# A diffusion backbone kernel: its beginning ordered by token tile instead of by column pair

## The chip, the cores and the metric

The program runs on one core of a Trainium2 chip, in one launch. The metric is the device time of one execution in microseconds (us), median over runs. All data are float32.

## The reference

Two layers over 256 latent tokens x and 256 context tokens, width 2048. Only the beginning of layer 0 matters here:

```
mod = silu(c) @ ada_w[0] + ada_b[0]            # shift, scale, gate, shift2, scale2, gate2, each 2048 wide
h_lat = rms_norm(x, norm_mix_g[0]) * (1 + scale) + shift
h_ctx = rms_norm(ctx, norm_mix_g[0]) * (1 + cscale) + cshift     # the same with silu(c_ctx)
q, k, v = h_lat @ attn_w_qkv                   # 2048 x 3072: 16 query heads, 4 key and 4 value heads of 128
k_c, v_c = h_ctx @ attn_w_qkv[:, 2048:]
```

Behind it follow grouped-query attention with rotary angles, the output projection, a squared-ReLU MLP (2048 to 8192 to 2048), and a second layer with a Fourier mixer and a second MLP.

## The kernel before

**Precision.** TensorE multiplies float32 operands in a reduced form, so each operand is split in two: a high half (`w_hi`, `h_hi`) written by ScalarE as a copy to that form, and a low half (`w_lo`, `h_lo`), written by VectorE as the difference. A product is three matmuls: high x high, low activation x high weight, high activation x low weight (`three`).

**Weights.** SP issues transfers of 1 MB ("pieces") into a ring `raw` of three. A piece is two slices; slice s is split by `split_hi(s)` on ScalarE (L712) and `split_lo(s)` on VectorE (L1197) into one of four slots (s % 4). A slot can be written again when its products are done: `slot_used` (L95) gives the number of products to wait for. The first three pieces cover two tiles of 128 rows of the weights (the K direction) and 1024 output columns each: slice 2p holds K tile 0 and slice 2p+1 K tile 1 of piece p.

**Products.** `product(r)` on TensorE (L1855) is one output block of 128 tokens x 512 columns over the K tiles of its group. `product_at(r)` (L106) gives (piece, column block, token tile). The first eight products are in the order (0,0,0), (0,0,1), (0,1,0), (0,1,1), (1,2,0), (1,2,1), (1,3,0), (1,3,1): both token tiles of a column block behind each other, so piece 0 serves products 0 to 3 and piece 1 products 4 to 7. Products 8 to 15 use piece 2, the last four for context tokens. Results are copied out of the banks by ScalarE (`first_copy`) or, for five of them, VectorE (`copy_first`).

**Modulation.** Two of the 16 column tiles of shift and scale are needed first. POOL issues the first four modulation transfers of 1 MB into `spare`; TensorE multiplies each (`first_piece`, 16 matmuls), ScalarE copies the rows (`rows_out(0)`), TensorE turns them to columns (`first_cols(0)`, 8 matmuls), VectorE adds bias and gain (`take_first(0, 0)`). The further modulation pieces wait until the context has landed (`load_start(4)`, L646).

**x.** ScalarE's queue issues both tiles of x, 128 tokens x 2048 each. ScalarE squares them (`square_in`), takes the root (`root_in`), VectorE normalises (`normed_in`) into `xn_in`. TensorE turns `xn_in` by 128 x 128 transposes. `turn_input(i)` turns column tiles 2i and 2i+1 of both token tiles into one bank (four transposes), and `x_out(i)` copies it to `xT`; numbers 0 to 5 come before the first product, 6 and 7 behind product 1. `shape(0, 0)` on ScalarE scales and shifts column tiles 0 and 1 for both token tiles and writes `h_hi`, `lower(0, 0)` on VectorE writes `h_lo`.

**Order.** Each engine executes its own list in order; semaphores join them, and there is no scheduler. ScalarE's list from the first copy on (L844 to L870) is: x_out 0, 1, rows_out(0), split 0, shape(0, 0), split 1, x_out 2 to 5, split 2, x_out 6, 7, first_copy 0, 1, split 3, first_copy 3, splits 4 and 5, then the squares of the two context tiles with their roots and first_copy(4) between them. TensorE turns the context's first columns (`turn_ctx(0)`) behind product 9. SP waits for the second modulation piece (L587) before it issues weights 0, 1, the context (2 MB) and weights 2.

Of the kernel before, what the change touches and what calls it, by code (L numbers as in the profile page):

```python
# [94 lines left out]
def slot_used(s):  # L95

    p = s // 2
    return products_before(p + 1) if p < 23 else 80
# [7 lines left out]
def product_at(r):  # L106

    p = max(p for p in range(24) if products_before(p) <= r)
# [20 lines left out]
X_BANK = (0, 1, 2, 3, 4, 5, 4, 5)  # L129
# [115 lines left out]
def layer_block(nc, x, c, ctx_in, c_ctx, ada_w, ada_b, norm_mix_g, norm_mlp_g, w_qkv, q_g, k_g, w_o,  # L245
# [125 lines left out]
    x_in = sem("x_in")  # L371
# [178 lines left out]
    def _(sp):  # L550
# [36 lines left out]
        sp.wait_ge(ada_in[start_slot(1)], 16)  # L587
        for p in range(24):
            if p < 6:
                load_first(p)  # L590
            else:
                load_columns(p, wqkv_v[p // 6, column_block(p)])
# [48 lines left out]
    def _(pool):  # L641
# [53 lines left out]
        for n in range(19):  # L695
            load_start(n)
# [14 lines left out]
    def _(act):  # L711
# [22 lines left out]
        for tt in range(2):  # L734
            act.dma_start(x_tm[:, tt, :], x[0, tt * P:(tt + 1) * P, :]).then_inc(x_in, 16)
# [8 lines left out]
        def square_in(st):  # L744

            if st < 2:
                act.wait_ge(x_in, 32)
# [3 lines left out]
            for b in range(4):  # L751
# [11 lines left out]
        for st in range(2):  # L763
            square_in(st)
            root_in(st)
        def x_out(i):

            act.wait_ge(x_T, i + 1)
            act.activation(xT[:, 2 * i:2 * i + 2, :], ps[:, X_BANK[i], :].rearrange("p (a t) -> p a t", a=2),
                           ACT.Copy).then_inc(x_T_out, 1)  # L770
# [23 lines left out]

        def first_copy(r):
# [4 lines left out]
            if r == 0:  # L800
                act.wait_ge(x_T, 8)
# [41 lines left out]

        x_out(0)  # L844
        x_out(1)
        rows_out(0)
        split_hi(0)
        shape(0, 0)
        split_hi(1)
        x_out(2)  # L850
        x_out(3)
        x_out(4)
        x_out(5)
        split_hi(2)
        x_out(6)
        x_out(7)
        first_copy(0)
        first_copy(1)
        split_hi(3)
# [336 lines left out]
    def _(dve):  # L1196
# [156 lines left out]

        def add_product(r):
# [70 lines left out]
        total_in(1)  # L1425
        normed_in(1)
# [5 lines left out]
        lower(0, 0)  # L1432
        split_lo(1)
        take_first(0, 1)
        split_lo(2)
        copy_first(2)
        split_lo(3)
# [405 lines left out]
    def _(pe):  # L1843
# [11 lines left out]
        def product(r):  # L1855
# [3 lines left out]
            if r < 5:  # L1859
                pe.wait_ge(x_T_out, (1, 2, 3, 4, 7)[r])  # L1860
            elif r == 33:
                pe.wait_ge(ctx_T_out, 7)
            else:
                pe.wait_ge(*flushed(bank_before(r)))
            hi, lo = (h_hi, h_lo) if tt < 2 else (hc_hi, hc_lo)
            pe.wait_ge(h_ready, 2 * c + 1 + tt // 2)
# [241 lines left out]
        def turn_input(i):  # L2108

            pe.wait_ge(xn_made, 3 + i // 4)  # L2110
            if i >= 6:
                pe.wait_ge(x_T_out, i - 1)
# [342 lines left out]
```

## Time and profile before

| what | value |
|---|---|
| median of three runs | 2008.24 us |
| lowest, highest | 2007.26, 2008.89 us |
| the profiled execution | 2007.61 us |
| its span, first to last instruction | 2005.8 us |
| TensorE busy | 1967.7 us, 98% |
| mean granted TensorE clock | 0.996 |
| VectorE, ScalarE busy | 1386.6, 969.4 us |
| HBM read | 535.91 MB |

The times in a profile count from the first instruction. A time line or a chain of waits gives start and duration; a bracket behind an instruction says how long its engine had been idle and what ended it. PE is TensorE's matmul, PEld its weight load, DVE VectorE, ACT ScalarE, POOL GpSimd. L numbers are lines of the kernel.

### The profile page before, as it was taken

The page shows a single profiled execution, that of the slowest core. Times are in us where ns is not written, and L with a number is a line of the kernel's source. Part 1 is how long each engine was busy: PE and PEld are TensorE (multiplying, and loading weights), DVE is VectorE, ACT ScalarE, POOL GpSimd, SP SyncE. Part 2 cuts the span into 40 slices and gives each one's busy share as a digit, 9 for nine tenths or more (in the row PEclk, how much of TensorE's full clock was granted, in tenths as well). Part 3 has the DMA queues.
Part 4 walks back from the last instruction along what each step waited for, and adds up shares of the span by engine and source line. Part 5 has one row for each costly group of instructions (what it writes and reads, how often), then busy time and mean ns, then how long its engine had stood idle before and what let it go on. Part 6 is the DMA issues. An engine that isn't in the chain of part 4 may idle for free.

```text
span 2005.8 us, 25016 instructions
## 1 busy us (share of the span) xinstructions
PE 1967.7 (98%) x10204; PEld 1609.2 (80%) x10204; DVE 1386.6 (69%) x1420; ACT 969.4 (48%) x1265; POOL 111.1 (6%) x196
## 2 busy tenths in 40 slices
PE   6999999999999999999999999999999999999998
PEld 4677756778888888888888788788888888888886
DVE  3666898879868787788878775766666455555456
ACT  6432565445544445544444454555554454444444
POOL 1111001100000000000000000000000000000000
PEclk9999999999999999999999999999999999999999
DMA  9998768769989899799999726577776566555653
GB/s 358 338 379 315 278 257 295 287 237 324 358 288 353 314 363 354 271 363 365 357 354 359 273 85 190 175 249 253 257 250 223 185 196 210 189 192 196 221 189 126
DMA packets 152261, 542.80 MB, mean 271 GB/s; under 512 B 9393, under 2 KB 10577, under 8 KB 114641
## 3 DMA queue, kind: packets, MB, share of 16 engines
q1 hardware_dynamic: 119312, 335.77, 47.7%
q0 software_dynamic: 31744, 201.34, 27.2%
q10 hardware_dynamic: 1090, 4.09, 0.5%
q8 instruction: 81, 1.33, 0.3%
q14 instruction: 34, 0.28, 0.0%
HBM read 535.91 MB, written 2.10 MB: 268 GB/s over the span
## 4 chain that ended last, share of the span: by engine, by line
PE 92%; DVE 3%; DMA 2%; ACT 1%; issue 1%; POOL 0%; ACTq 0%; DVEq 0%; POOLq 0%
PE ps L2098 13%; PE ps L2032 11%; PE ps L2036 11%; PE ps L2035 11%; PE ps L2096 11%; PE ps L2099 6%; PE ps L1848 6%; PE ps L2095 6%; PE ps L1849 5%; PE ps L1850 5%; PE ps L2257 1%; PE ps L2204 1%; PE ps L1913 1%; DMA spare<-in_ada_w 1%; PE ps L2242 1%
## 5 line engine op out<-in xcount | busy, mean ns | idle before, releaser
L1201 DVE TENSOR_TENSOR w_lo<-raw,w_hi 128x1024 fp32r<-128x1024 f32 x616 | 749.3, 1223 | 472.2 <-ACT w_hi L727 472.0
L727 ACT ACTIVATE w_hi<-raw 128x1024 fp32r<-128x1024 f32 x616 | 649.2, 1059 | 848.1 <-PE ps L2036 345.8
L2098 PE MATMUL ps<-hh,w_hi 128*128 128x512 f32 x1088 | 426.9, 398 | 1.7 <-DVE hh L1627 1.7
L2032 PE MATMUL ps<-w_hi,hh 128*128 128x512 f32 x992 | 386.1, 389 | 1.5 <-DVE w_lo L1201 1.5
L2035 PE MATMUL ps<-w_lo,hh 128*128 128x512 f32 x992 | 386.0, 389 | 0.0
L2036 PE MATMUL ps<-w_hi,hh 128*128 128x512 f32 x992 | 385.9, 389 | 0.0
L2096 PE MATMUL ps<-hh,w_hi 128*128 128x512 f32 x960 | 379.9, 396 | 0.0
L2099 PE MATMUL ps<-hh,w_lo 128*128 128x256 f32 x1088 | 302.8, 278 | 0.0
L2095 PE MATMUL ps<-hh,w_lo 128*128 128x256 f32 x960 | 267.5, 279 | 0.0
L2099 PEld LDWEIGHTS ps<-hh,w_lo 128*128 128x128 f32 x1088 | 205.3, 189 | 40.8
L2032 PEld LDWEIGHTS ps<-w_hi,hh 128*128 128x128 f32 x992 | 186.2, 188 | 40.5 <-DVE w_lo L1201 1.9
L2036 PEld LDWEIGHTS ps<-w_hi,hh 128*128 128x128 f32 x992 | 186.2, 188 | 38.8
L2035 PEld LDWEIGHTS ps<-w_lo,hh 128*128 128x128 f32 x992 | 186.2, 188 | 38.5
L2098 PEld LDWEIGHTS ps<-hh,w_hi 128*128 128x128 f32 x1088 | 206.9, 190 | 11.6 <-issue 5.5
L2095 PEld LDWEIGHTS ps<-hh,w_lo 128*128 128x128 f32 x960 | 180.2, 188 | 43.7
L1229 DVE SCALAR_TENSOR_TENSOR ada_sum<-ada_raw,silu,ada_sum 128x2048 f32<-128x2048 f32 x83 | 194.7, 2346 | 2.0 <-DMA ada_raw<-in_ada_w 1.9
L1848 PE MATMUL ps<-w_hi,hh 128*128 128x512 f32 x448 | 191.2, 427 | 3.1 <-DVE hh L1351 1.6
L2096 PEld LDWEIGHTS ps<-hh,w_hi 128*128 128x128 f32 x960 | 180.0, 187 | 0.0
L1849 PE MATMUL ps<-w_lo,hh 128*128 128x512 f32 x448 | 175.8, 392 | 0.0
L1850 PE MATMUL ps<-w_hi,hh 128*128 128x512 f32 x448 | 175.2, 391 | 0.0
L693 POOL DMA_DIRECT2D ada_raw<-in_ada_w x132 | 70.9, 537 | 1150.6 <-DVE ada_sum L1229 586.0
L1848 PEld LDWEIGHTS ps<-w_hi,hh 128*128 128x128 f32 x448 | 84.5, 189 | 38.6 <-issue 13.9
(252 smaller groups left out, 1618.4 us busy)
## 6 DMA issues: line engine op xcount, KB each, us to landing
raw<-in_mlp_w SPq DMA_DIRECT2D x256, 1024.0 KB, 5.4
ada_raw<-in_ada_w POOLq DMA_DIRECT2D x151, 1024.0 KB, 6.0
spare<-in_ada_w POOLq DMA_DIRECT2D x29, 1024.0 KB, 7.0
raw<-in_attn_w_qkv SPq DMA_DIRECT2D x24, 1024.0 KB, 10.4
raw<-in_attn_w_o SPq DMA_DIRECT2D x16, 1024.0 KB, 7.7
raw<-in_fourier_w_o SPq DMA_DIRECT2D x16, 1024.0 KB, 5.1
g_row<-in_ada_w POOLq DMA_DIRECT2D x12, 1024.0 KB, 9.0
g_row<-gate_rows SPq DMA_DIRECT2D x48, 64.0 KB, 5.2
```

Of the source, the lines that this page charges most:

```text
L727: act.activation(w_slot(s)[0], raw[:, piece % RAW, s % 2, :], ACT.Copy).then_inc(hi_ready, 1)
L1201: nc.vector.tensor_tensor(lo, raw[:, s // 2 % RAW, s % 2, :], hi.bitcast(F32), ALU.subtract).then_inc(lo_ready, 1)
L1848: mm(dst, w_h, m_h, start=start, stop=False, skip_group_check=True)
L1849: mm(dst, w_h, m_l, start=False, stop=False, skip_group_check=True)
L1850: return mm(dst, w_l, m_h, start=False, stop=stop, skip_group_check=True)
L2032: ins = mm(bank_of(tt, nb), h_hi[:, k % KT, tok], hi[:, cols], start=start, stop=False)
L2035: mm(bank_of(tt, nb), h_hi[:, k % KT, tok], lo[:, cols], start=False, stop=False)
L2036: return mm(bank_of(tt, nb), h_lo[:, k % KT, tok], hi[:, cols], start=False, stop=stop)
L2095: mm(ps[:, bank, 0:T], w_lo[:, s % SPLIT, w], h_hi[:, k, :], start=False, stop=False, skip_group_check=True)
L2096: ins = mm(both, w_hi[:, s % SPLIT, w], hh[:, k, :, :], start=False, stop=(k == KT - 1), skip_group_check=True)
L2098: mm(both, w_hi[:, s % SPLIT, w], hh[:, k, :, :], start=(k == 0), stop=False, skip_group_check=True)
L2099: ins = mm(ps[:, bank, 0:T], w_lo[:, s % SPLIT, w], h_hi[:, k, :], start=False, stop=(k == KT - 1), skip_group_check=True)
```

## The change

The second tile of x is issued on POOL's queue behind the first four modulation transfers; each tile of x has a semaphore of its own. SP waits for the fourth modulation transfer before the first weights, and for the sixth before weights 3. x is turned by token tile: `turn_x_in(tt, j)` turns column tiles 4j to 4j+3 of one token tile; the first tile's four calls come behind modulation piece 1, the second tile's behind products 1 and 3. Shaping and low half are made by token tile too (`shape_first`, `lower_first`). Products 0 to 3 are the four column blocks of token tile 0, products 4 to 7 those of tile 1; slots 0 and 1 are free after six products. ScalarE's and VectorE's lists are reordered accordingly.

```diff
--- before.py
+++ after.py
@@ -95,6 +95,8 @@
 def slot_used(s):
 
     p = s // 2
+    if p == 0:
+        return 6
     return products_before(p + 1) if p < 23 else 80
 
 
@@ -105,6 +107,8 @@
 
 def product_at(r):
 
+    if r < 8:
+        return TILE_FIRST[r]
     p = max(p for p in range(24) if products_before(p) <= r)
     j = r - products_before(p)
     if p >= 6:
@@ -126,7 +130,12 @@
     return max(m for m in range(r) if product_bank(m) == product_bank(r))
 
 
-X_BANK = (0, 1, 2, 3, 4, 5, 4, 5)
+TILE_FIRST = ((0, 0, 0), (0, 1, 0), (1, 2, 0), (1, 3, 0), (0, 0, 1), (0, 1, 1), (1, 2, 1), (1, 3, 1))
+
+
+def turned_x_bank(tt, j):
+
+    return j if tt == 0 else (5, 7)[j % 2]
 
 
 def group_tiles(c):
@@ -368,7 +377,9 @@
     ada_in = [sem(f"ada_in{i}") for i in range(11)]
     c_in = sem("c_in")
     small_in = sem("small_in")
-    x_in = sem("x_in")
+    x_in = [sem(f"x_in{i}") for i in range(2)]
+    first_hi = sem("first_hi")
+    first_h = sem("first_h")
     ctx_rows_in = sem("ctx_rows_in")
     rope_in_sem = sem("rope_in_sem")
     dft_in_sem = sem("dft_in_sem")
@@ -584,8 +595,10 @@
                                  gate_rows[v != 0][32 * j:32 * j + 32, :]).then_inc(gate_in, 16)
 
         sp.dma_start(ident[:, :], ident_in).then_inc(c_in, 16)
-        sp.wait_ge(ada_in[start_slot(1)], 16)
+        sp.wait_ge(ada_in[start_slot(3)], 16)
         for p in range(24):
+            if p == 3:
+                sp.wait_ge(ada_in[start_slot(5)], 16 * start_count(5))
             if p < 6:
                 load_first(p)
             else:
@@ -692,7 +705,10 @@
                 pool.wait_ge(slice_done, 2 * P_DOWN[0] - QKV + 128)
             pool.dma_start(ring(vector_slot(i)), ada_v[lay][m, i % KT]).then_inc(ada_in[vector_slot(i)], 16)
 
-        for n in range(19):
+        for n in range(4):
+            load_start(n)
+        pool.dma_start(x_tm[:, 1, :], x[0, P:2 * P, :]).then_inc(x_in[1], 16)
+        for n in range(4, 19):
             load_start(n)
         load_vector(0)
         load_vector(1)
@@ -731,8 +747,7 @@
 
         act.dma_start(vec_rows[0:16, 3, :], c[0].rearrange("(t p) -> t p", p=P)).then_inc(c_in, 16)
         act.dma_start(vec_rows[16:32, 3, :], c_ctx.rearrange("(t p) -> t p", p=P)).then_inc(c_in, 16)
-        for tt in range(2):
-            act.dma_start(x_tm[:, tt, :], x[0, tt * P:(tt + 1) * P, :]).then_inc(x_in, 16)
+        act.dma_start(x_tm[:, 0, :], x[0, 0:P, :]).then_inc(x_in[0], 16)
         for l in range(2):
             act.dma_start(vec_rows[0:96, l, :], ada_b[l].rearrange("(t p) -> t p", p=P)).then_inc(small_in, 16)
         act.dma_start(vec_rows[0:32, 2, :], norm_mix_g.rearrange("l (t p) -> (l t) p", p=P)).then_inc(small_in, 16)
@@ -741,14 +756,14 @@
         act.activation(sig[:, :], misc[:, 0:32], ACT.Sigmoid).then_inc(sig_ready, 1)
         act.wait_ge(eps_set, 4)
 
-        def square_in(st):
+        def square_in(st, blocks=range(4)):
 
             if st < 2:
-                act.wait_ge(x_in, 32)
+                act.wait_ge(x_in[st], 16)
             else:
                 act.wait_ge(ctx_rows_in, 16)
             src = x_tm if st < 2 else c_rows
-            for b in range(4):
+            for b in blocks:
                 j = 4 * st + b
                 if j >= 2:
                     act.wait_ge(xs_done, j - 1)
@@ -760,14 +775,14 @@
             act.activation(rst_in[:, st, 1:2], rst_in[:, st, 0:1], ACT.Sqrt,
                            bias=eps_col[:, 1:2]).then_inc(xroot_ready, 1)
 
-        for st in range(2):
-            square_in(st)
-            root_in(st)
-        def x_out(i):
-
-            act.wait_ge(x_T, i + 1)
-            act.activation(xT[:, 2 * i:2 * i + 2, :], ps[:, X_BANK[i], :].rearrange("p (a t) -> p a t", a=2),
-                           ACT.Copy).then_inc(x_T_out, 1)
+        square_in(0)
+        root_in(0)
+
+        def x_out(tt, j):
+
+            act.wait_ge(x_T, 4 * tt + j + 1)
+            act.activation(xT[:, 4 * j:4 * j + 4, tt * P:(tt + 1) * P],
+                           ps[:, turned_x_bank(tt, j), :].rearrange("p (a t) -> p a t", a=4), ACT.Copy).then_inc(x_T_out, 1)
 
         def rows_out(c):
 
@@ -792,13 +807,23 @@
             act.wait_ge(mod_done, shaped[0])
             act.activation(dst[:, kts, :], src[:, kts, :], ACT.Copy).then_inc(hhi_ready, 1)
 
+        def shape_first(tt):
+
+            tok = slice(tt * P, (tt + 1) * P)
+            act.wait_ge(a_ready, 1)
+            act.wait_ge(x_T_out, 4 * tt + 1)
+            for kt in range(2):
+                act.activation(xT[:, kt, tok], xT[:, kt, tok], ACT.Identity, bias=mod_col[:, kt:kt + 1],
+                               scale=a_col[:, 0, kt:kt + 1]).then_inc(mod_done, 1)
+            shaped[0] += 2
+            act.wait_ge(mod_done, shaped[0])
+            act.activation(h_hi[:, 0:2, tok], xT[:, 0:2, tok], ACT.Copy).then_inc((first_hi, hhi_ready)[tt], 1)
+
         def first_copy(r):
 
             if r in FIRST_ON_VECTOR:
                 return
             p, cb, tt = product_at(r)
-            if r == 0:
-                act.wait_ge(x_T, 8)
             if r == 9:
                 act.wait_ge(ctx_T, 8)
             act.wait_ge(prod_done, r + 1)
@@ -841,22 +866,24 @@
                 dst = qT[:, 4 * b:4 * b + 4, tt * P:(tt + 1) * P]
             act.activation(dst, src, ACT.Copy).then_inc(head_T_out, 1)
 
-        x_out(0)
-        x_out(1)
+        for j in range(4):
+            x_out(0, j)
         rows_out(0)
+        square_in(1, range(2))
+        shape_first(0)
         split_hi(0)
-        shape(0, 0)
         split_hi(1)
-        x_out(2)
-        x_out(3)
-        x_out(4)
-        x_out(5)
+        square_in(1, range(2, 4))
+        root_in(1)
         split_hi(2)
-        x_out(6)
-        x_out(7)
+        x_out(1, 0)
+        shape_first(1)
+        x_out(1, 1)
+        split_hi(3)
         first_copy(0)
+        x_out(1, 2)
         first_copy(1)
-        split_hi(3)
+        x_out(1, 3)
         first_copy(3)
         split_hi(4)
         split_hi(5)
@@ -1351,6 +1378,13 @@
             nc.vector.tensor_tensor(lo[:, kts, :], src[:, kts, :], hi[:, kts, :].bitcast(F32),
                                     ALU.subtract).then_inc(h_ready, 1)
 
+        def lower_first(tt):
+
+            tok = slice(tt * P, (tt + 1) * P)
+            dve.wait_ge((first_hi, hhi_ready)[tt], 1)
+            nc.vector.tensor_tensor(h_lo[:, 0:2, tok], xT[:, 0:2, tok], h_hi[:, 0:2, tok].bitcast(F32),
+                                    ALU.subtract).then_inc((first_h, h_ready)[tt], 1)
+
         def add_product(r):
 
             p, cb, tt = product_at(r)
@@ -1422,19 +1456,20 @@
 
         total_in(0)
         normed_in(0)
-        total_in(1)
-        normed_in(1)
         for i, (dst, w) in enumerate(((bias_col[:, 0:96], 96), (bias_col[:, 96:192], 96), (misc[:, 32:96], 64))):
             dve.wait_ge(vec_T, 3)
             nc.vector.tensor_copy(dst, ps[:, 7, i * P:i * P + w]).then_inc(vec_ready, 1)
         take_first(0, 0)
         split_lo(0)
-        lower(0, 0)
+        lower_first(0)
         split_lo(1)
+        total_in(1)
+        normed_in(1)
+        split_lo(2)
+        lower_first(1)
+        split_lo(3)
         take_first(0, 1)
-        split_lo(2)
         copy_first(2)
-        split_lo(3)
         split_lo(4)
         split_lo(5)
         total_in(2)
@@ -1856,14 +1891,17 @@
 
             p, cb, tt = product_at(r)
             c = r // 16
-            if r < 5:
-                pe.wait_ge(x_T_out, (1, 2, 3, 4, 7)[r])
+            if r < 4:
+                pe.wait_ge(x_T_out, r + 1)
             elif r == 33:
                 pe.wait_ge(ctx_T_out, 7)
-            else:
+            elif r > 4:
                 pe.wait_ge(*flushed(bank_before(r)))
             hi, lo = (h_hi, h_lo) if tt < 2 else (hc_hi, hc_lo)
-            pe.wait_ge(h_ready, 2 * c + 1 + tt // 2)
+            if r < 4:
+                pe.wait_ge(first_h, 1)
+            else:
+                pe.wait_ge(h_ready, 2 * c + 1 + tt // 2)
             tok = slice((tt % 2) * P, (tt % 2 + 1) * P)
             kts = group_tiles(c)
             n = kts.stop - kts.start
@@ -2105,16 +2143,16 @@
         pe.wait_ge(silu_ready, 1)
         pe.wait_ge(ones_set, 1)
 
-        def turn_input(i):
-
-            pe.wait_ge(xn_made, 3 + i // 4)
-            if i >= 6:
-                pe.wait_ge(x_T_out, i - 1)
-            for k in range(2):
-                for tt in range(2):
-                    f = 2 * i + k
-                    ins = nc.tensor.transpose(ps[:, X_BANK[i], k * T + tt * P:k * T + (tt + 1) * P], xn_in[:, tt, f * P:(f + 1) * P],
-                                              ident[:, :])
+        def turn_x_in(tt, j):
+
+            pe.wait_ge(xn_made, 2 * tt + j // 2 + 1)
+            if (tt, j) == (1, 1):
+                pe.wait_ge(vec_ready, 3)
+            if tt == 1 and j >= 2:
+                pe.wait_ge(x_T_out, 3 + j)
+            for k in range(4):
+                f = 4 * j + k
+                ins = nc.tensor.transpose(ps[:, turned_x_bank(tt, j), k * P:(k + 1) * P], xn_in[:, tt, f * P:(f + 1) * P], ident[:, :])
             ins.then_inc(x_T, 1)
 
         first_piece(0)
@@ -2122,14 +2160,11 @@
         pe.wait_ge(small_in, 64)
         for i, n in enumerate((96, 96, 64)):
             nc.tensor.transpose(ps[:, 7, i * P:i * P + n], vec_rows[0:n, i, :], ident[0:n, 0:n]).then_inc(vec_T, 1)
+        for j in range(4):
+            turn_x_in(0, j)
         first_piece(2)
-        turn_input(0)
-        turn_input(1)
         first_piece(3)
-        turn_input(2)
         first_cols(0)
-        for i in range(3, 6):
-            turn_input(i)
 
         def turn_ctx(i):
 
@@ -2150,9 +2185,9 @@
 
         for r in range(77):
             product(r)
-            if r == 1:
-                turn_input(6)
-                turn_input(7)
+            if r in (1, 3):
+                turn_x_in(1, r - 1)
+                turn_x_in(1, r)
             if 9 <= r < 12:
                 turn_ctx(2 * r - 18)
                 turn_ctx(2 * r - 17)
```

## Rows read from the trace of the kernel before

**Rows 1.** The page: span, busy time of the engines, the chain by engine.
```profile
span 2005.8 us, 25016 instructions
...
PE 1967.7 (98%) x10204; PEld 1609.2 (80%) x10204; DVE 1386.6 (69%) x1420; ACT 969.4 (48%) x1265; POOL 111.1 (6%) x196
...
PE 92%; DVE 3%; DMA 2%; ACT 1%; issue 1%; POOL 0%; ACTq 0%; DVEq 0%; POOLq 0%
```

**Rows 2.** The chain of waits, 20 to 50 us: start us, us, what.
```profile
4.07 18.79 DMA spare<-in_ada_w
...
22.90 1.47 PE ps L1887 x16
...
26.34 0.17 DVE a_col L1321
...
32.20 0.43 PE ps L1848
...
36.23 0.23 PE ps L1849
...
38.58 2.00 ACT w_hi L727 x2
40.59 2.45 ACT sq_in L755 x8
...
44.04 2.46 ACT sq_in L755 x8
...
47.23 1.12 DVE c_rows L1309
...
48.40 1.09 PE ps L2146 x8
```

**Rows 3.** Busy time by stretch: bounds, length, engines, granted clock, transfers' share, GB/s.
```profile
0.00:15.00 15.00, 2.24 (x17) 0.87 (x17) 1.52 (x11) 5.04 (x11) 3.88 (x8) 1.00 0.85 298
15.00:20.00 5.00, 3.94 (x31) 1.65 (x35) 3.08 (x7) 3.35 (x11) 0.00 (x0) 1.00 1.03 350
20.00:25.00 5.00, 4.65 (x36) 2.51 (x28) 0.70 (x4) 1.79 (x4) 0.00 (x0) 1.00 1.02 394
...
31.00:34.00 3.00, 3.00 (x8) 2.33 (x8) 1.23 (x1) 1.12 (x2) 0.78 (x1) 0.52 1.01 406
```

**Rows 4.** TensorE in order of time: start us, us, instruction, [idle before].
```profile
20.67 1.97 PE L2116 MATMUL ps<-ident,xn_in 128*128 128x128 f32 x8
...
29.11 0.47 PE L1848 MATMUL ps<-w_hi,hh 128*128 128x512 f32 x1 [1.64 <-DVE hh L1351]
...
34.27 1.04 PE L2116 MATMUL ps<-ident,xn_in 128*128 128x128 f32 x8
...
39.23 0.50 PE L1848 MATMUL ps<-w_hi,hh 128*128 128x512 f32 x1 [0.49 <-DVE w_lo L1201]
```

**Rows 5.** Transfers issued at 15.77 and 16.71 us: count, size, us to landing.
```profile
raw<-in_attn_w_qkv SPq DMA_DIRECT2D x1, 1024.0 KB, 8.5
...
c_rows<-in_ctx SPq DMA_DIRECT2D x1, 2048.0 KB, 16.2
```

**Rows 6.** ScalarE by line and shape, 20 to 62 us: xcount | busy, mean ns.
```profile
L727 ACT ACTIVATE w_hi<-raw 128x1024 fp32r<-128x1024 f32 x8 | 8.4, 1059 | 0.0
...
L769 ACT ACTIVATE xT<-ps 128x512 f32<-128x512 f32 x8 | 4.3, 594 | 6.3 <-PE ps L2116 6.3
...
L789 ACT ACTIVATE xT<-xT,mod_col,a_col 128x256 f32<-128x256 f32 x2 | 1.1, 594 | 0.6 <-DVE a_col L1321 0.6
```

**Rows 7.** The same view, 200 to 300 us: halves of width 256 on ScalarE and VectorE.
```profile
L948 ACT ACTIVATE hh<-ps 128x256 fp32r<-128x256 f32 x4 | 1.5, 376 | 0.4 <-PE ps L2257 0.4
...
L1544 DVE TENSOR_TENSOR hh<-ps,hh 128x256 fp32r<-128x256 f32 x4 | 1.7, 418 | 0.0
```

**Rows 8.** VectorE by line and shape, 20 to 62 us.
```profile
L1201 DVE TENSOR_TENSOR w_lo<-raw,w_hi 128x1024 fp32r<-128x1024 f32 x8 | 9.7, 1221 | 2.7 <-ACT w_hi L727 2.7
...
L1309 DVE TENSOR_SCALAR xn_in<-x_tm,rst_in 128x1024 f32<-128x1024 f32 x1 | 0.7, 748 | 0.0
```

## The prediction

> **What bounds the kernel now.** I read the page first. The span is 2005.8 us, TensorE has work in 98% of it, and 92% of the chain that ended last is TensorE [rows 1]. So what is lost before its first products, or between them, is hardly won back later. The change touches only the first 60 us. There the chain of waits has two parts [rows 2]. Up to 22.9 us it is a transfer: the fourth piece of modulation weights (issued at 4.07, landed at 22.9). Then come its matmuls, the copy of the rows, the columns, the shaping of x and the halves of the first weights. Later, from 38.58 to 48.40, the chain leaves TensorE: ScalarE splits slices 4 and 5, squares the context's eight blocks, VectorE normalises, and at 48.40 TensorE can turn the context. That is 9.8 us from the first split, 7.8 from the end of the second (40.59). This second part is what the reader should hold on to: whatever starts split 4 later moves the turning by as much.
>
> The bytes come next [rows 3]: the transfers run at the full share from 4 us on, and they move 298 GB/s over the first 15 us, 350 up to 20 and 394 up to 25. Last, TensorE in order of time [rows 4]: eight transposes take 1.97 us at 20.67 and 1.04 at 34.27; the first product waits until 29.11; slice 3 costs only 0.49 us of waiting at 39.23.
>
> **The transfers.** One transfer is 1.05 MB. The fourth piece needs four pieces, one tile of x and 0.2 MB of small loads ahead of it: 5.4 MB. By rows 3, 4.47 MB are there at 15 us and 0.350 MB come per us, so it lands at about 17.8 (was 22.9); I take 18.2, because the second tile of x, which moved at a high rate, is no longer among these bytes. The second tile follows in the same queue: 6.5 MB, about 20.8. The SP queue now waits for the fourth piece and not for the second, so its first weights are issued at 18.2 and not at 15.8. Landing took 8.5 us from issue [rows 5], which would make 26.7; but ahead of that landing the same seven transfers are on the way as before, and by the sum of the bytes they are there at 24.3, as now. I take 24.3 and keep 26.7 as the upper end. The context (issued at 16.7, 16.2 us to landing [rows 5]: 32.9) stays, for the same reason. The piece at which SP now waits again before its fourth weights costs nothing: these weights are used behind the context's squares.
>
> The Trainium skill, "DMA: Bandwidth & Descriptors", section "Issuing engines are not separate DMA queues", says that transfers of all issuing engines run on the same 16 engines and interleave. By it, the new order can bring nothing forward of the bytes that the first weights stand behind: 24.3, and a t0 (below) of 27.1; by the row alone it would be 29.5. It speaks against much gain from the transfers.
>
> **Up to the first product.** TensorE turns the first tile (16 transposes) ahead of pieces 2 and 3; this takes 1.9 us at the faster pace of rows 4 and 3.9 at the slower, all while it waits for piece 3 anyway if the faster holds. From piece 3's first matmul (22.90) to the shaping factors (26.5) it was 3.6 us [rows 2]: factors at 21.8. ScalarE however has two blocks of the second tile's squares ahead of the shaping, waiting for that tile: 20.8 + 1.2 = 22.0. The shaping of half the width (two activations of 0.4, one copy of 0.38, by the 256 wide ones of 0.59 and 0.38 [rows 6, 7]) ends at 23.2. The first split waits for its weights: 24.3 + 1.05 = 25.35; low half + 1.22 [rows 8] = 26.6; the low half of h, 0.42 [rows 7], stands behind it in VectorE's order: t0, the first product, = 27.1, 2.0 earlier than 29.11. If TensorE is slow before, t0 is 28.1; with the late weights 29.5.
>
> **Two products, then a stall.** TensorE now stands idle from about 21.5 to 27.1. After an idle time of 1.6 us (with 0.5 more behind it) the granted clock was 0.52 in the stretch from 31 to 34 [rows 3], the level of 1.2 GHz: matmuls came every 0.43 us and not every 0.23 [rows 2], eight of them, 1.6 us lost. So I take nine of the first twelve at 0.43 and three at 0.23: products 0 and 1 end at 31.7. Only then does TensorE turn the first two quarters of tile 1. ScalarE stands in order behind that: quarter out (32.2 to 32.75, 0.59 each [rows 6], 0.5 in a stream), shaping of tile 1 (1.15), second quarter (0.5), and only then split 3 (1.05): 35.5; its low half on VectorE: 36.75. Product 2 needs slice 3 for its second half, since by tile it now comes after two products and not after four. TensorE has its transposes and product 2's first half done at 33.35 and waits 3.4 us, where it waited 0.49 before.
>
> Behind it are nine matmuls (products 2 and 3), eight transposes, and twelve matmuls (products 4 and 5). At 0.23 and 0.12 each: 2.1 + 0.9 + 2.8 = 5.8, so 42.55. With a slow stretch like the one in rows 2 and 3 it is 1.6 more: 44.1. With all nine matmuls and the transposes slow: 45.3. I take 44.1, since 3.4 us of idling is twice what the trace shows ahead of a fall. Splits 4 and 5 must now wait for six products (slices 0 and 1 are read until product 5), where four were enough: 44.1 + 2.0 = 46.1, against 40.59. **This is +5.5 us** on the second part of the chain: the turning of the context goes from 48.40 to 53.9.
>
> TensorE cannot hide it: products 6 and 7 end at 46.9, product 8 with slice 5 at 48.3, a piece (1.0) and product 9 (1.4) at 50.7, then 3.2 us of waiting. Before, 0.2 us. Behind it TensorE is again the chain, and again the clock may fall: between 0 and 1.6 us, and I take 0.8, half of the only row there is.
>
> What is moved at no cost: normalising tile 1 (0.75 per half [rows 8]) behind the second low half, hidden by the slow products; the same number of copies, squares and halves on each engine; the smaller vector loads (in the queue behind one tile of x only, so they land sooner).
>
> Sum: 5.5 + 0.8 = 6.3 on the profiled execution's 2007.61 us (span 2005.8): 2013.9. That execution stands 0.63 below the median 2008.24, so the forecast is 2014.5.
>
> **The rivals.**
> A, as above, with the clock falling in at least one of the two new gaps: 2012.3 to 2017. For it: rows 2 and 3 show a fall after less idling. Chance 0.55.
> B, the same stalls, but the clock stays: 42.55 + 2.0 is 4.0 after 40.59, less up to 1.3 if the first twelve matmuls are fast as well: 2.7 to 4.0, so 2011 to 2012.2. For it: the matmul at 29.11, right behind 1.6 us of idling, is not among the slow ones. Chance 0.28.
> C, not slower: the stall does not come, because the quarters of tile 1 are turned and out before product 2's first half is done, so that slice 3 is ready by 33.35 at the latest. Then TensorE runs through: 27.1 + 36 matmuls (8.3) + 16 transposes (1.9) + 0.5 = 37.8, where split 4 started at 38.58: 0.8 less, 2007.4, at most 2.0 less. It decides from an end of split 3 at 32.1, and by my count that is 3.4 us away. Against it: ScalarE's order. Chance 0.10.
> D, the change does not do what it says: the fourth piece is not sooner by much, because its queue was slow by itself, and the weights that now wait for it come 2.4 us later. All that follows moves: 2016 to 2019. Against it: the rate of rows 3. Chance 0.07.
>
> A difference under 0.2% (4.0 us) can hardly be told from none; slower by over that begins at 2012.3. A and D lie above, B and C at or below: slower 0.60 (0.02 off A and D at their edge, none from B), same 0.36, faster 0.04, since no mechanism that I see gives 4 us. The range 2008.5 to 2017.5 leaves out most of C and the top of D; A's own range is 2012.3 to 2017.
>
> **What would show it.** Right: fourth piece landed near 18, first weights near 24.3, first product near 27; a wait of 3 us for slice 3's low half near 34 to 37, with the granted clock near 0.5 around both gaps; splits 4 and 5 from 44; the first turning of the context near 54 with a wait ahead. Wrong: split 4 before 41, or no wait at the context; or a saving behind 60 us of the size of the loss, which rows 1 leave little room for.

## The result, and the profile after

The changed kernel takes 2017.86 us (median of 4 runs, 2015.91 to 2018.42) beside 2008.13 (2007.26 to 2008.89, 4 runs) for the kernel before: a ratio of 1.005, interval 1.0038 to 1.0062. It is slower by 9.7 us; the forecast was 6.3 us slower, and the measured time lies 0.36 above the top of its range. The profiled execution took 2017.72.

The page shows the span and the busy time that answer to [rows 1]. TensorE is busy 3.3 us longer, and the span is 10.1 us longer; so most of what came is waiting, and only a part is slower clock.

```profile
span 2015.9 us, 25024 instructions
...
PE 1971.0 (98%) x10204; PEld 1611.8 (80%) x10204; DVE 1386.4 (69%) x1421; ACT 970.6 (48%) x1268; POOL 112.1 (6%) x197
```

The chain of waits over the first 60 us answers to [rows 2] (start us, us, what). It starts with the second tile of x, and not with a piece of weights. The line to hold beside the old one is the split at 45.85: it is the later of splits 4 and 5, which [rows 2] have at 38.58 together.

```profile
4.94 16.90 DMA x_tm<-in_x
...
24.44 1.06 ACT w_hi L743
...
32.46 0.61 ACT xT L784
...
33.15 0.89 ACT xT L816 x2
...
34.96 0.95 ACT w_hi L743
35.94 1.24 DVE w_lo L1228
...
45.85 1.04 ACT w_hi L743
46.90 2.46 ACT sq_in L770 x8
...
54.36 1.44 PE ps L2181 x8
55.80 1.87 PE ps L1925 x16
```

TensorE in order of time answers to [rows 4]; in brackets stands the idle time before, and what ended it. Of its three gaps the first, 4.89, stands where 1.64 stood; the other two, 3.66 and 2.30, are new. The last line is product 12, the first product of the next stage, which I use below as a clock for the whole beginning. It starts at 59.01 in the kernel before (the second fence) and at 66.55 here: 7.54 later.

```profile
27.19 0.77 PE L1883 MATMUL ps<-w_hi,hh 128*128 128x512 f32 x1 [4.89 <-DVE hh L1385]
...
37.22 0.50 PE L1883 MATMUL ps<-w_hi,hh 128*128 128x512 f32 x1 [3.66 <-DVE w_lo L1228]
...
54.36 1.44 PE L2181 MATMUL ps<-ident,c_rows 128*128 128x128 f32 x8 [2.30 <-DVE c_rows L1336]
...
66.55 0.50 PE L1883 MATMUL ps<-w_hi,hc 128*128 128x512 f32 x1
```

```profile
59.01 0.50 PE L1848 MATMUL ps<-w_hi,hc 128*128 128x512 f32 x1
```

ScalarE in order of time shows where the middle gap comes from. It waits 2.89 for the first turned quarter of tile 1, moves it out, shapes it, moves the second quarter out, and only then splits slice 3 (34.86).

```profile
32.46 0.60 ACT L784 ACTIVATE xT<-ps 128x512 f32<-128x512 f32 x1 [2.89 <-PE ps L2155]
33.15 0.88 ACT L816 ACTIVATE xT<-xT,mod_col,a_col 128x128 f32<-128x128 f32 x2
34.06 0.42 ACT L820 ACTIVATE hh<-xT 128x256 fp32r<-128x256 f32 x1
34.38 0.58 ACT L784 ACTIVATE xT<-ps 128x512 f32<-128x512 f32 x1
34.86 1.05 ACT L743 ACTIVATE w_hi<-raw 128x1024 fp32r<-128x1024 f32 x1
...
44.89 2.01 ACT L743 ACTIVATE w_hi<-raw 128x1024 fp32r<-128x1024 f32 x2 [1.19 <-PE ps L1885]
```

The stretches have the columns of [rows 3]; the granted clock is the third number from the end. Three stretches lie around and behind the gaps, and the last is far behind, where nothing was changed. Below it is the same place in the kernel before, moved by the delay.

```profile
27.00:31.00 4.00, 3.81 (x9) 3.06 (x10) 3.60 (x7) 1.91 (x5) 0.00 (x0) 0.50 1.02 426
...
37.00:41.00 4.00, 3.78 (x11) 2.90 (x12) 1.09 (x4) 0.00 (x0) 0.00 (x0) 0.61 1.01 349
54.00:58.00 4.00, 3.64 (x25) 2.04 (x26) 2.35 (x4) 2.96 (x5) 0.00 (x1) 0.62 0.48 179
1290.00:1302.00 12.00, 8.72 (x39) 7.25 (x38) 10.99 (x22) 7.99 (x14) 0.00 (x0) 0.72 0.28 88
```

```profile
1283.00:1295.00 12.00, 8.97 (x47) 7.78 (x48) 10.99 (x23) 8.26 (x15) 0.00 (x0) 0.86 0.28 89
```

The transfer of the first weights (issued at 19.36) took this long to land, where [rows 5] have 8.5:

```profile
raw<-in_attn_w_qkv SPq DMA_DIRECT2D x1, 1024.0 KB, 5.1
```

**Where the 10.1 us of the span come from.** I followed the same matmul through both traces. It is 7.54 late at product 12, and this stays as it is up to 130 us. A wait for a modulation piece makes it 8.3 from 141 to 195 us. It is 7.75 late from there to 1110, 7.88 at 1280 and 9.21 at 1315. So three quarters arise ahead of 60 us, as forecast. The step of 1.33 is the stretch at 1290: the clock is low for twice as long there (mean 0.72 over 12 us, that is 3.4 us of full clock lost; before 0.86 and 1.7). The last 0.9 comes at 1987 us: weights of the MLP landed late, ScalarE waited 1.71 for them, and TensorE then 0.59 for their low half, where the kernel before has no wait on TensorE. In after_again, the same program once more, this step is 0.4, and it is none in e6_delay.

```profile
1984.67 2.01 ACT L743 ACTIVATE w_hi<-raw 128x1024 fp32r<-128x1024 f32 x2 [1.71 <-DMA raw<-in_mlp_w]
1987.04 0.50 PE L2070 MATMUL ps<-w_hi,hh 128*128 128x512 f32 x1 [0.59 <-DVE w_lo L1228]
```

### The profile page after: what moved, and what is told of

Read it like the earlier page. It is cut to its first block, busy times and chain, and to the rows that moved or that the text cites. A ratio compares the mean times of both kernels' runs of the same rounds, so it can differ in the third digit from the quotient of the medians.

```text
span 2015.9 us, 25024 instructions
## 1 busy us (share of the span) xinstructions
PE 1971.0 (98%) x10204; PEld 1611.8 (80%) x10204; DVE 1386.4 (69%) x1421; ACT 970.6 (48%) x1268; POOL 112.1 (6%) x197
## 3 DMA queue, kind: packets, MB, share of 16 engines
q8 instruction: 81, 1.33, 0.3%
## 4 chain that ended last, share of the span: by engine, by line
PE 92%; DVE 3%; DMA 2%; ACT 2%; issue 1%; POOL 0%; ACTq 0%; DVEq 0%; POOLq 0%
PE ps L2136 13%; PE ps L2134 11%; PE ps L2070 11%; PE ps L2074 11%; PE ps L2073 11%; PE ps L2137 6%; PE ps L1883 6%; PE ps L2133 6%; PE ps L1884 5%; PE ps L1885 5%; PE ps L2292 1%; PE ps L2239 1%; PE ps L1951 1%; DMA x_tm<-in_x 1%; PE ps L2277 1%
```

## The experiments

The theory: in ScalarE's order split 3 stands behind two quarters and the shaping of tile 1; so product 2 waits for slice 3, splits 4 and 5 wait for six products, and the context behind them comes too late for TensorE. Its rival: the loss is the transfers' new order or the low clock by itself. A second rival: what happens ahead of 60 us does not reach the end of the span. "Before" is always the kernel before on the same chip, in the same set of runs (medians 2007.82, 2007.86, 2007.81 and 2007.16).

**e1_split3**: split 3 directly behind split 2, on both engines.

```diff
         split_hi(2)
+        split_hi(3)
         x_out(1, 0)
         shape_first(1)
         x_out(1, 1)
-        split_hi(3)
         first_copy(0)
```

(and on VectorE split_lo(3) ahead of lower_first(1)).

> The changed kernel with split 3 moved ahead of the turning of tile 1's first quarter on ScalarE, and its low half ahead of tile 1's on VectorE. Theory 1 (the stall is ScalarE's order, and it sets the split of slices 4 and 5 and by it the context): slice 3 is ready at about 32.5, no wait of 3.7 us inside product 2, six products at about 39.5 (44.9), first turning of the context at about 49 (54.4), and the whole 4.5 to 6.5 us under the changed kernel, 2011 to 2013.5. Rival 2 (transfers: the later issue of the weights costs the time): split 3 finds no weights at 29.5 and all stays, 2017 to 2018.5. Rival 3 (the context's chain is not what decides): the stall goes, but at most its own 3.7 us comes back.

Measured: 2009.20 (12 runs, 2005.56 to 2016.08), ratio 1.0009, interval 0.9999 to 1.002: +1.4. ScalarE in order of time, then TensorE:

```profile
40.28 2.01 ACT L743 ACTIVATE w_hi<-raw 128x1024 fp32r<-128x1024 f32 x2 [1.17 <-PE ps L1885]
```

```profile
49.76 1.97 PE L2181 MATMUL ps<-ident,c_rows 128*128 128x128 f32 x8 [2.31 <-DVE c_rows L1336]
...
61.96 0.50 PE L1883 MATMUL ps<-w_hi,hc 128*128 128x512 f32 x1
```

TensorE no longer waits for slice 3; splits 4 and 5 start at 40.28 and not at 44.89, the context is turned 4.60 earlier, and product 12 comes 4.59 earlier. The wait ahead of the context stays (2.31): it belongs to the distance from split 4 to the context, which this edit does not touch. The median came 1.8 us below the expected 2011: the profile gives back 4.59 ahead of 60 us, the medians 7.2 against after_again.

**e3_ctx_early**: the context's first tile squared and normalised ahead of splits 4 and 5; split 3 stays late.

```diff
         first_copy(0)
+        square_in(2)
+        root_in(2)
         x_out(1, 2)
         ...
         split_hi(5)
-        square_in(2)
-        root_in(2)
         first_copy(4)
```

(and on VectorE total_in(2) and normed_in(2) ahead of split_lo(4)).

> The changed kernel with only the context's first tile squared and normalised ahead of splits 4 and 5, in the 5.2 us in which ScalarE is idle. The stall inside product 2 stays at 3.7 us. Theory 1: six products at 44.9 as before, the context's turning at about 51.2 to 52 instead of 54.4 without a wait worth naming, and no slow clock behind it: 2.3 + 1.6 = about 4 us under the changed kernel, 2013 to 2014.5. Rival 3 (the context's chain does not decide): no difference, 2017.9.

Measured: 2010.71 (11 runs, 2008.43 to 2012.28), ratio 1.0015, interval 1.0006 to 1.0024: +2.9. TensorE in order of time:

```profile
37.21 0.50 PE L1883 MATMUL ps<-w_hi,hh 128*128 128x512 f32 x1 [3.66 <-DVE w_lo L1228]
...
51.76 1.03 PE L2181 MATMUL ps<-ident,c_rows 128*128 128x128 f32 x8
...
62.31 0.50 PE L1883 MATMUL ps<-w_hi,hc 128*128 128x512 f32 x1
```

The stall of 3.66 is all there, and still product 12 is 4.24 earlier than in the changed kernel. So the stall by itself is not the whole loss. It is not free either: product 12 is still 3.30 later than in the kernel before, and 2.70 later than in e2_both below, where the stall is gone too. The two in series, stall and late context, cost 7.5; with either one alone about 3 is left. The median is again lower than expected (2013 to 2014.5).

**e2_both**: both edits.

> As the run before, and besides the squares, root and normalising of the context's first tile moved ahead of splits 4 and 5 (behind first_copy(0)). Theory 1: no wait ahead of the context's turning, which comes at about 47 to 48, so the beginning is 0 to 1.5 us shorter than before the change: 2006.5 to 2009. Rival 2: 2014 or more. If the context's chain does not decide, it equals the run with split 3 alone.

Measured: 2008.69 (11 runs, 2006.58 to 2010.99), ratio 1.0007, interval 0.9998 to 1.0016: +0.9, product 12 at 59.61. Both gaps are gone, and yet there is no gain over the kernel before. ScalarE and TensorE now wait for transfers:

```profile
48.73 1.06 ACT L743 ACTIVATE w_hi<-raw 128x1024 fp32r<-128x1024 f32 x1 [2.22 <-DMA raw<-in_attn_w_qkv]
```

```profile
57.93 1.75 PE L1925 MATMUL ps<-ada_raw,silu 128*32 128x256 f32 x16 [1.31 <-DMA ada_raw<-in_ada_w]
```

The weights that ScalarE waits for are those that SP's second wait holds back; the modulation piece that TensorE waits for was issued at 45.88, behind them, and landed at 57.88. Behind this wait of 1.31 the clock fell again (0.57 in the stretch from 58 to 62). I had put SP's wait at nothing, because these weights were used behind the late context; with the context early, that cover is gone.

**e7_no_second_wait**: e2_both without it.

```diff
-            if p == 3:
-                sp.wait_ge(ada_in[start_slot(5)], 16 * start_count(5))
```

> The run with split 3 and the context's squares both moved (e2_both), without SP's wait for the sixth modulation piece ahead of weights 3. In e2_both that wait left transfers idle: ScalarE waited 2.2 us for weights 3 and TensorE 1.3 us for the eighth modulation piece at 57.9, with a slow stretch of the clock behind. If that wait costs, both go, product 12 comes at 57.9 to 58.2 instead of 59.6 and the time is 1.5 to 3 us under e2_both, 1 to 2 under the kernel before. If weights 3 now take the transfers' time from the modulation pieces 4 to 6, TensorE waits for those at 44 to 51 and it is no faster.

Measured: 2007.45 (11 runs, 2005.58 to 2009.38), ratio 0.9998, interval 0.9989 to 1.0006: −0.4. Product 12 at 57.88: 1.73 earlier than in e2_both, and 1.13 earlier than in the kernel before. The median moved by 1.3, a little less than expected and within what these runs can tell.

```profile
57.88 0.50 PE L1881 MATMUL ps<-w_hi,hc 128*128 128x512 f32 x1
```

**after_again**: the changed kernel once more, beside the next two.

> The changed kernel once more, for its spread beside the kernel before. The first 60 us cost 7.5 us (product 12 at 66.55 and not at 59.01); the rest of the 9.7 us first measured is one more slow stretch of the clock near 1300 us and a late transfer. If these are chance, the median of many runs is 7.5 to 8.5 us over the kernel before and single runs lie from 5 to 11 over it; if they follow from the change, it is 9 to 10 again.

Measured: 2016.44 (5 runs, 2016.2 to 2017.84), ratio 1.0046, interval 1.0034 to 1.0058: +8.6. The loss is the same within the intervals; it lies between the two expectations (up to 8.5, and from 9) and does not decide between them. The middle gap is again 3.66 long, but the clock behind it is 1.00 in the stretch from 37 to 41 us and not 0.61; the first product came 0.7 later, and product 12 at 66.39.

**e5_order**: the product order by tile alone, in the kernel before: first tile and shaping, transfers and SP's wait stay as they were.

```diff
+    if p == 0:
+        return 6
     return products_before(p + 1) if p < 23 else 80
...
+    if r < 8:
+        return TILE_FIRST[r]
```

(and on VectorE the copy of product 2 behind the low half of slice 3, which product 2 now needs). Without this second edit, in e5_order_alone, the program stands still and has no time: the copy waits for product 2, and product 2 for the low half that stands behind the copy.

> The kernel before with only the order of its first eight products changed to that of the change (slots 0 and 1 free after six products; VectorE's copy of product 2 behind slice 3's low half, which product 2 now needs); transfers, turning and shaping as before. Theory 1: slice 3 is needed at 35.8 and ready at 39.2, a wait of 3.4 us inside product 2; six products done at 44 to 46 instead of four at 38; splits 4 and 5 and the context 5.5 to 7 us later; with a slow clock behind the second wait 5.5 to 8.5 us in all. Rival 2 (the loss comes with the transfers or the turning by tile): under 2 us over the kernel before.

Measured: 2014.45 (6 runs, 2010.88 to 2019.54), ratio 1.0036, interval 1.0023 to 1.005: +6.6. TensorE in order of time, then the stretch behind the gap:

```profile
39.89 0.50 PE L1854 MATMUL ps<-w_hi,hh 128*128 128x512 f32 x1 [3.22 <-DVE w_lo L1207]
...
54.55 1.09 PE L2152 MATMUL ps<-ident,c_rows 128*128 128x128 f32 x8 [2.31 <-DVE c_rows L1315]
...
66.74 0.50 PE L1854 MATMUL ps<-w_hi,hc 128*128 128x512 f32 x1
```

```profile
40.00:44.00 4.00, 4.00 (x18) 3.29 (x19) 0.69 (x1) 0.60 (x1) 0.00 (x0) 1.00 1.03 348
```

The order of the products alone, over ScalarE's old order, makes the same two gaps and puts product 12 at 66.74. Some 0.6 of its 7.73 is a first product that came later in this profile (29.75 for 29.11). So the order is enough to lose the time; it is not the only part that does, as the next run shows.

**e4_old_transfers**: the changed kernel with the old transfers: both tiles of x in ScalarE's queue, SP waiting for piece 2 and for nothing later.

```diff
-        sp.wait_ge(ada_in[start_slot(3)], 16)
+        sp.wait_ge(ada_in[start_slot(1)], 16)
...
-        pool.dma_start(x_tm[:, 1, :], x[0, P:2 * P, :]).then_inc(x_in[1], 16)
```

> The changed kernel with the transfers of the kernel before: both tiles of x on ScalarE's queue, SP waiting for the second modulation piece only and not again at weights 3. Everything else as in the changed kernel. Theory 1 (first product = first weights at 24.3 plus split and halves): the fourth piece lands at 22.9 again, shaping factors at 26.5, shaping of tile 0 to 27.7, split 0 to 28.7, halves to 30.4: first product at 30.5 instead of 27.2, and all behind it 3.3 us later, 3 us over the changed kernel. If the transfers' order gives nothing (the skill's rule on shared engines alone, with the weights at 24.3 in both), it equals the changed kernel.

Measured: 2020.11 (5 runs, 2017.14 to 2020.41), ratio 1.0058, interval 1.0046 to 1.007: +12.2. TensorE in order of time, then the transfer of the first weights, issued at 15.71:

```profile
30.25 0.76 PE L1879 MATMUL ps<-w_hi,hh 128*128 128x512 f32 x1 [4.39 <-DVE hh L1381]
...
39.85 0.65 PE L1879 MATMUL ps<-w_hi,hh 128*128 128x512 f32 x1 [3.66 <-DVE w_lo L1224]
```

```profile
raw<-in_attn_w_qkv SPq DMA_DIRECT2D x1, 1024.0 KB, 8.5
```

The new order of transfers is a gain: without it the first product comes 3.06 later than in the first profile of the change (2.36 later than in after_again) and the time is 3.7 us higher than that of after_again.

Beside e5_order, which has the same transfers and the same product order, this run shows the third part of the change, the turning by token tile with its lists on ScalarE and VectorE: 5.7 us by the medians, 2.44 by product 12. The stall ends at the same time in both (39.85 and 39.89). Behind it e4_old_transfers has eight transposes of tile 1 (0.8 us), which e5_order has not, and the low clock, which e5_order did not have in its profile (1.6). Splits 4 and 5, e5_order and then this run:

```profile
45.07 2.01 ACT L733 ACTIVATE w_hi<-raw 128x1024 fp32r<-128x1024 f32 x2 [2.19 <-PE ps L1856]
```

```profile
47.47 2.01 ACT L738 ACTIVATE w_hi<-raw 128x1024 fp32r<-128x1024 f32 x2 [1.16 <-PE ps L1881]
```

By product 12 the change is then 7.7 for the order, 2.4 for the turning by tile and 2.6 to 2.8 back for the transfers. One profile of each cannot tell how much of the 2.4 is the chance of the clock.

**e6_delay**: the kernel before with all its first transfers held back, by four fills of a spare row on VectorE, so that c is turned at 12.26 and not at 3.05. If the second rival held, the end would not see these 9.2 us.

> The kernel before with all engines held at the start until VectorE has cleared one unused buffer four times (about 2 us each, 7.5 to 8.5 us in all); nothing else is changed. It asks whether a delay of the beginning as such goes through to the end one to one, or is caught up or multiplied. One to one: the median is 7.5 to 9 us over the kernel before, as the changed kernel's 8.6. If a later start by itself brings further slow stretches of the clock or late transfers, 9 or more; if the transfers catch up, under 6.

Measured: 2017.54 (5 runs, 2016.99 to 2019.57), ratio 1.0054, interval 1.0042 to 1.0067: +9.7, for product 12 at 67.50 (+8.49). A delay ahead of 60 us comes through whole; the second rival falls. The median is 0.7 above the 9 us that one to one allowed; the low clock near 1290 was the long one here (3.4 us lost). The first product is 10.04 late and product 12 only 8.49, because the slow stretch of the kernel before did not come behind the same gap, which the expectation did not have.

```profile
39.15 0.47 PE L1856 MATMUL ps<-w_hi,hh 128*128 128x512 f32 x1 [1.65 <-DVE hh L1359]
```

```profile
41.00:44.00 3.00, 3.00 (x19) 2.57 (x18) 1.22 (x1) 1.77 (x4) 2.55 (x3) 1.00 1.03 400
```

**e8_filled** and **e9_before_filled**: the gap ahead of the first product filled with transposes that nobody reads, 32 in e7_no_second_wait, 12 in the kernel before.

```diff
             turn_input(i)
+        pe.wait_ge(vec_ready, 3)
+        for k in range(12):
+            nc.tensor.transpose(ps[:, 7, (k % 4) * P:(k % 4 + 1) * P], ..., ident[:, :])
```

> e7_no_second_wait with 32 transposes of tile 0 of x into an unused bank behind the modulation's columns, where TensorE stands idle for 4.8 us ahead of the first product; their results are read by nobody. If the slow clock of the first products (3.4 us of slow clock lost between 24 and 32 us) comes from that idling, products 0 and 1 take 2.8 us and not 4.6, product 12 comes 1 to 1.7 us sooner than 57.9, and the time is 1 to 2 us under e7_no_second_wait, 2005.5 to 2006.5. If the transposes run at half pace they end at 29.6 and it is 2 us slower. If ScalarE's list from 33 on decides instead, nothing changes.

> The kernel before with 12 such transposes in the 1.64 us of idling ahead of its first product; nothing else is changed. If that idling is what lowers the clock from 30.3 to 33.9, product 12 comes at 57.3 and not at 59.0, and the time is 1.7 us under the kernel before. If the fall is set by the lighter load from 25 to 31 as a whole, or the context's chain or the transfers' end decide product 12, no difference.

Measured: e8_filled 2006.57 (11 runs, 2004.19 to 2008.01), ratio 0.9995, interval 0.9986 to 1.0003: −1.2. e9_before_filled 2006.40 (11 runs, 2004.35 to 2007.91), ratio 0.9993, interval 0.9984 to 1.0002: −1.4. In e8_filled the first product comes as early as in the changed kernel, at 27.09, at full clock, but two waits for transfers stand behind it (0.74 at 44.01, and 1.51). Product 12 is 0.78 later than in e7_no_second_wait, where 1 to 1.7 earlier was expected:

```profile
27.09 0.47 PE L1881 MATMUL ps<-w_hi,hh 128*128 128x512 f32 x1 [1.09 <-DVE hh L1383]
...
52.54 1.07 PE L1923 MATMUL ps<-g_row,silu 128*32 128x256 f32 x16 [1.51 <-DMA g_row<-in_ada_w]
...
58.66 0.50 PE L1881 MATMUL ps<-w_hi,hc 128*128 128x512 f32 x1
```

In e9_before_filled no slow stretch is left ahead of 60 us (TensorE, then the stretch that [rows 3] have at 0.52):

```profile
29.06 0.47 PE L1848 MATMUL ps<-w_hi,hh 128*128 128x512 f32 x1 [0.34 <-issue]
...
57.68 0.50 PE L1848 MATMUL ps<-w_hi,hc 128*128 128x512 f32 x1
```

```profile
31.00:34.00 3.00, 3.00 (x18) 2.54 (x18) 1.23 (x1) 1.77 (x4) 0.64 (x1) 1.00 1.01 403
```

Product 12 comes 1.33 earlier, and only that: the early first product of the change brings nothing beyond it, since with TensorE free of gaps the transfers are next.

**e9_again** and **e8_again**: the two best once more.

> e9_before_filled once more. Its product 12 came 1.3 us sooner than in the kernel before, and its median was 1.4 us lower with an interval from 3.2 us lower to 0.4 higher. If the early slow stretch is what was saved, the second set again has a median 1 to 2 us under the kernel before; if the first set was chance, 0.

> e8_filled once more: median again 0.5 to 2 us under the kernel before if its sooner product 12 (0.4 us) and the missing early slow stretches are real, 0 if not; it is not expected to beat e9, since it waits 2.3 us for modulation pieces.

Measured: e9_again 2005.93 (11 runs, 2004.80 to 2007.75) beside 2007.16, ratio 0.9993, interval 0.9985 to 1.0002: −1.2. e8_again 2006.76 (12 runs, 2003.96 to 2009.35), ratio 0.9998, interval 0.9989 to 1.0006: −0.4. The kernel before with its gap filled was lower than the kernel before in both sets, by 1.2 and 1.4 us, about the size of its removed slow stretch (1.7 us), though product 12 was only 1.3 and 0.8 earlier. For e8 the second set (−0.4) does not bear out the expected 0.5 to 2. Each interval just reaches 1; so e9 points to a small gain and does not settle it.

**All of them by one number.** The start of product 12 in one profile of each set, beside 59.01 in the only profile of the kernel before, and the median over the kernel before of the same set, both as differences in us:

| kernel | product 12 | median |
|---|---|---|
| e4_old_transfers | +10.2 | +12.2 |
| e6_delay | +8.5 | +9.7 |
| e5_order | +7.7 | +6.6 |
| changed kernel, two sets | +7.5, +7.4 | +9.7, +8.6 |
| e3_ctx_early | +3.3 | +2.9 |
| e1_split3 | +3.0 | +1.4 |
| e2_both | +0.6 | +0.9 |
| e8_filled, two sets | −0.4, −0.6 | −1.2, −0.4 |
| e7_no_second_wait | −1.1 | −0.4 |
| e9_before_filled, two sets | −1.3, −0.8 | −1.4, −1.2 |

The order is nearly kept, and the distance between the two columns is at most 2.2 us, with both signs. That is of the size of slow stretches that come and go behind 60 us.

## Why the prediction was right in kind and too small

The forecast was 6.3 us on the profiled execution, and its span grew by 10.1. The 3.8 that are missing stand in three places: 0.5 in the late context, 0.8 in the clock behind the third gap, and 2.6 behind product 12, where the forecast had nothing. The last is the largest, and without it the time would have been inside the range.

**The transfers: right.** Fourth piece forecast at 18.2, landed at 19.35; second tile 20.8 and 21.85. Each is 1.1 late. The row of the first 15 us has 284 GB/s where [rows 3] have 298: 4.26 MB there and not 4.47, which is 0.6 us at the forecast's rate. The rest of it I did not trace.

```profile
0.00:15.00 15.00, 3.85 (x33) 1.46 (x33) 3.11 (x14) 5.65 (x12) 4.43 (x9) 1.00 0.85 284
```

First weights: forecast at 24.3 by the sum of the bytes, measured 24.4 (5.1 after the issue at 19.36; ScalarE starts to split them at 24.44). The issue-to-landing row alone (8.5) would have given 26.7. The Trainium skill, "DMA: Bandwidth & Descriptors", section "Issuing engines are not separate DMA queues", says that the transfers of all issuing engines share the same 16 engines and interleave. The trace agrees: issued 3.6 us later, the first weights landed at the same time (24.4 for 24.3), with the same bytes ahead of them. The forecast took this to speak against much gain from the transfers; the gain came all the same, by the earlier fourth piece. e4_old_transfers has the 8.5 back.

**Up to the first product: right.** Forecast 27.1, measured 27.19, with the factors at 22.7 for 21.8. This hit is partly luck: the forecast had the shaping done at 23.2, 1.1 ahead of the weights. The second tile of x and its squares made it 24.42, the moment at which the weights landed, so that all of this room was used up, and the chain above goes through x. Products 0 and 1 ended at 31.8 (31.7), at the low clock.

**The stall for slice 3: right, slightly small.** Forecast 3.4 us with product 2's second half at 36.75, measured 3.66 and 37.22. The six products ended at 44.85 (44.1), splits from 44.89. The assumed slow stretch behind the stall was there in this profile (0.61) and not in after_again. e1_split3 shows the cause that the forecast named: move split 3, and the wait is gone.

**The late context: right in mechanism.** Turning forecast at 53.9, measured 54.36; so +5.96 in place of +5.5: the splits began 0.8 later than forecast, and the way from them to the turning was 0.3 shorter (9.47 for 9.8). The forecast wait of 3.2 is 2.30: the work ahead of it ended later by more than the turning did.

**The step that failed in size: the third gap's clock.** "Between 0 and 1.6 us, and I take 0.8". From the turning to product 12 it is 10.61 us in the kernel before and 12.19 here: 1.58, the upper end (0.62 in the stretch from 54 to 58). All five profiles with this gap (2.30 or 2.31) have a slow stretch there, e1_split3, e4_old_transfers, e5_order and after_again too; e3_ctx_early, where the gap is gone, has none. The forecast itself had the gap at 3.2, twice the 1.64 ahead of the only fall in [rows 2, 3]; half of that row's 1.6 was no reasoned value.

**The term that failed most: nothing behind 60 us.** "The change touches only the first 60 us", and so the sum ended there. Measured there: +7.54 for +6.3. Behind it the profile shows +2.6 more, 1.3 of it from a low clock at 1290 that lasted twice as long and 0.9 from the late weights at 1987. This is no effect of the change that I could show: 3.4 us are lost there in after_again, e1_split3, e7_no_second_wait, e6_delay and e8_filled as well, 1.7 in the kernel before, e2_both, e3_ctx_early, e4_old_transfers, e8_again and both profiles of e9, and none in e5_order. e8_filled and e8_again are one kernel. Whether a shift of the whole program makes the long one likelier stays open; e6_delay, a pure shift, lost 1.2 us more than its product 12. The range should have had room for it: the kernel before alone spread over 2003.7 to 2010.9 in the later sets. The second median of the changed kernel, 2016.44, lies inside the range, so being 0.36 above it in the first set is in part chance.

**The rivals.** A was the case that came, 0.9 above its own range by the first median and inside it by after_again's difference (+8.6 on 2008.24 is 2016.8). B fell with the low clock in all three gaps, though after_again shows that it held for the middle one. C fell: split 3 ended at 35.9, and C needed 32.1. D fell: the piece came 3.5 us sooner, and the weights were not late.

## What to carry to other kernels

When products are put in another order, go through the orders of the engines that feed them, item by item: a split that stood early enough for four products was too late when it was needed after two, and everything queued behind it went along. Work for the next stage (here the context's squares) belongs ahead of the items that wait for the present one: moved there it took back 5.7 of 8.6 us by the medians, 4.2 of 7.5 by product 12, with the stall itself still in place. And count the low clock behind every gap that a change opens, in full, as an end of the range.

## What the runs showed of the hardware

The length of an idle time did not decide whether TensorE's clock fell to 1.2 GHz behind it. Ahead of the first product 1.64 us idle (then 0.50 more) brought 0.52 in the kernel before; 1.65 (then 0.51) brought none in e6_delay, where TensorE had done the same work before it; 1.64 in e5_order brought one again. Behind the middle gap 3.66 us brought 0.61 in the changed kernel and 1.00 in after_again, the same program; 3.22 in e5_order brought none. The shorter gap ahead of the context, 2.30 or 2.31, brought a fall in all five profiles that have it, and so did the 4.4 to 4.9 us ahead of the first product in seven of seven. Each fall took 1.7 us of full clock, or twice that. What of it lies in idle time costs nothing: of the 3.4 around the first product about 2 fell on work (0.50 from 27 to 31 us). With the gap filled with transposes that nobody reads, the fall did not come (e8_filled, e9_before_filled, both again in their second sets).

A delay of a few microseconds at the start goes through a program of 2000 us undiminished (e6_delay: 8.5 at product 12, 9.7 at the end). The stages behind it gave back 0.5 up to 1280 us, and the longer low clock at 1290 took 1.4.
